# Sample rows in two groups of four and sample state updates four steps behind, in the gated linear attention heads of a two-layer decoder trunk

## The reference

```python
q_dec = q * jnp.exp(bcum); k_state = k * jnp.exp(blast - bcum)
o_intra = jnp.einsum('nbhij,nbhje->nbhie', att, v)
def step(s, inp):
    qc, kc, vc, dc = inp
    o_inter = jnp.einsum('bhid,bhde->bhie', qc, s)
    s = dc[..., None] * s + jnp.einsum('bhjd,bhje->bhde', kc, vc)
    return s, o_inter
...
y = (o * jax.nn.silu(z.astype(F32))).astype(h.dtype) @ w_out      # o after its own RMS norm
```

## Time and profile before

| | |
|---|---|
| runs | 1653.91 us median of 3 (1651.29, 1653.91, 1654.04) |
| profiled execution | span 1651.1 us; no separate time of it is listed, the lowest run is 1651.29 |
| PE busy | 1613.4 us, 98% |
| DVE busy | 818.7 us, 50% |
| ACT busy | 458.2 us, 28% |
| POOL busy | 375.8 us, 23% |
| chain that ended last | PE 94%, DVE 3%, SP's queue, DMA and ACT 1% each |
| mean granted TensorE clock | 0.990 of full speed |

### The profile page before, as it was taken

How to read it: one execution, slowest core, us unless ns; L and a number is a source line. 1 busy time by engine, 2 the same in 40 slices (tenths; PEclk the granted TensorE clock), 3 DMA queues, 4 the chain that set the end, 5 groups by cost and what they waited for, 6 DMA issues and landing times.

```text
span 1651.1 us, 25118 instructions
## 1 busy us (share of the span) xinstructions
PE 1613.4 (98%) x9827; PEld 1501.1 (91%) x9827; DVE 818.7 (50%) x1271; ACT 458.2 (28%) x969; POOL 375.8 (23%) x384
## 2 busy tenths in 40 slices
PE   6999999999999999998999999999999999999996
PEld 5899999999999999998788898888998989979896
DVE  4654449443944475457224562245622356224475
ACT  4321112111211121123325413154040541315423
POOL 3022212211211212211314223133130322314310
PEclk8999999999999999998999999999999999999998
DMA  9512221221122121210202212022120221201312
GB/s 330 193 56 87 62 63 42 84 74 42 55 78 64 57 67 54 77 41 27 64 18 73 84 40 77 13 64 84 53 66 12 64 96 40 77 13 40 110 37 108
DMA packets 137545, 115.03 MB, mean 70 GB/s; under 512 B 6013, under 2 KB 120281, under 8 KB 137442
## 3 DMA queue, kind: packets, MB, share of 16 engines
q1 hardware_dynamic: 135616, 112.87, 22.0%
q10 hardware_dynamic: 1834, 0.74, 0.2%
HBM read 99.05 MB, written 15.00 MB: 69 GB/s over the span
## 4 chain that ended last, share of the span: by engine, by line
PE 94%; DVE 3%; SPq 1%; DMA 1%; ACT 1%; issue 0%; ACTq 0%; DVEq 0%
PE psA L549 40%; PE psB L549 29%; PE psB L1804 8%; PE psA L1804 4%; PE psB L1860 2%; PE psB L1877 2%; PE psX L1842 2%; PE psB L1868 2%; PE psX L1897 1%; DVE a_hi L637 1%; PE psB L1909 1%; PE psX L1720 1%; DMA ada<-in_ada_w 1%; DVE y_rows L1606 0%; PE psB L1910 0%; PE psX L1661 0%
## 5 line engine op out<-in xcount | busy, mean ns | idle before, releaser
L344 POOL TENSOR_TENSOR w_lo<-stage,w_hi 128x1024 fp32r<-128x1024 f32 x100 | 249.7, 2496 | 891.1 <-ACT w_hi L339 891.1
L339 ACT ACTIVATE w_hi<-stage 128x1024 fp32r<-128x1024 f32 x100 | 107.0, 1070 | 433.7 <-PE psB L549 297.6
L549 PE MATMUL psA<-h_hi,w_hi 128*128 128x362 f32 (+1 forms) x864 | 210.9, 349 | 4.1 <-DVE h_lo L453 3.8
L549 PE MATMUL psA<-h_lo,w_hi 128*128 128x362 f32 (+1 forms) x864 | 193.6, 329 | 0.0
L549 PE MATMUL psA<-h_hi,w_lo 128*128 128x362 f32 (+1 forms) x864 | 193.1, 329 | 0.0
L549 PEld LDWEIGHTS psA<-h_hi,w_hi 128*128 128x128 f32 x864 | 151.4, 190 | 27.1 <-issue 21.2
L549 PEld LDWEIGHTS psA<-h_hi,w_lo 128*128 128x128 f32 x864 | 151.5, 190 | 0.0
L549 PEld LDWEIGHTS psA<-h_lo,w_hi 128*128 128x128 f32 x864 | 151.4, 190 | 0.0
L549 PE MATMUL psA<-a_hi,w_hi 128*128 128x362 f32 (+1 forms) x480 | 109.7, 334 | 2.6 <-DVE a_lo L640 1.9
L549 PE MATMUL psB<-h_hi,w_hi 128*128 128x362 f32 (+1 forms) x480 | 109.7, 331 | 0.0
L549 PE MATMUL psB<-h_hi,w_lo 128*128 128x362 f32 (+1 forms) x480 | 107.9, 327 | 0.0
(11 more groups left out here) (345 smaller groups left out, 2790.6 us busy)
## 6 DMA issues: line engine op xcount, KB each, us to landing
stage<-in_gla_w_in SPq DMA_DIRECT2D x40, 512.0 KB, 3.8
stage<-in_pool_w_in SPq DMA_DIRECT2D x32, 512.0 KB, 4.1
ada_stage<-in_ada_w SPq DMA_DIRECT2D x24, 512.0 KB, 3.8
ada<-in_ada_w SPq DMA_DIRECT2D x16, 512.0 KB, 8.4
stage<-in_pool_w_out SPq DMA_DIRECT2D x16, 512.0 KB, 3.4
v<-in_state_gla SPq DMA_DIRECT2D x32, 256.0 KB, 2.6
out_new_gla_sample<-v SPq DMA_DIRECT2D x32, 256.0 KB, 2.1
stage<-in_gla_w_out SPq DMA_DIRECT2D x16, 512.0 KB, 3.7
```

The source lines that it names most:

```text
L339: nc.scalar.activation(slot_hi(plan, j), stage[:, j % 2, :], ACT.Copy).then_inc(lay.hi_done, 1)
L344: nc.gpsimd.tensor_tensor(slot_lo(plan, j), stage[:, j % 2, :], slot_hi(plan, j).bitcast(f32), ALU.subtract).then_inc(lay.lo_done, 1)
L549: last = nc.tensor.matmul(ps[u][:, t, 0:width], weight(w[:, p, :], k), a[:, k, n0:n0 + width], start=(k == 0 and pas == 0), stop=(k == kt ...
```

## The change

The rows of the sample sequences are made four at a time, at s = 4 and s = 8, with all four loads waited for first. `sample_update`, `ks_rows` and `sample_state` of sequence b move from step b+2 to step b+4. Those of the last three sequences leave the scan: on PE they stand behind steps k = 0, 2 and 4 of Z3, on DVE around `gate_product(0)` and `(1)`. `sample_out` is split: its first part stays at s = 9, its second part and the release of the unit stand behind Z3's step 0. The second `mean_square(8)` goes from behind step 1 to behind step 3. Stores follow on SP.

```diff
@@ SP
-                    if s >= 2:
-                        store_state(s - 2)
+                    if 4 <= s <= NSUP:
+                        store_state(s - 4)
+                    if s == NSUP + 1:
+                        for b in range(NB - 3, NB):
+                            store_state(b)
@@ DVE
-                for s in range(NSUP + 2):
-                    if s >= 2:
-                        ks_rows(s - 2)
+                for s in range(NSUP + 1):
+                    if s >= 4:
+                        ks_rows(s - 4)
...
-                    if s >= 2:
-                        sample_state(s - 2)
-
+                    if s >= 4:
+                        sample_state(s - 4)
+
+                ks_rows(NB - 3)
+                sample_state(NB - 3)
+                ks_rows(NB - 2)
+                dve.wait_ge(smp_o_evac, g + 1)
+                gate_product(0)
+                sample_state(NB - 2)
+                ks_rows(NB - 1)
+                gate_product(1)
+                sample_state(NB - 1)
                 dve.wait_ge(s0_ready, (g + 1) * NB)
                 dve.wait_ge(o_evac, (g + 1) * NSUP)
                 dve.sem_inc(L1.evac[1], 1)
-                dve.wait_ge(smp_o_evac, g + 1)
-                gate_product(0)
-                gate_product(1)
                 dve.wait_ge(orms_ready, g + 1)
@@ PE
-                    if s >= 3:
-                        pe.wait_ge(s0_ready, g * NB + s - 2)
+                    if s >= 5:
+                        pe.wait_ge(s0_ready, g * NB + s - 4)
...
-                    for b in (b0, b0 + 1):
+                    for b in range(b0, b0 + 4):
                         pe.wait_ge(s0_loaded[b % 4], g * 32 + (b // 4) * 16 + 16)
+                    for b in range(b0, b0 + 4):
...
-                    if b + 2 < NSUP:
-                        pe.wait_ge(S_ready, g * NSUP + b + 3)
+                    if b + 4 < NSUP:
+                        pe.wait_ge(S_ready, g * NSUP + b + 5)
...
-                    if s in (2, 4, 6, 8):
-                        sample_inter(s - 2)
+                    if s in (4, 8):
+                        sample_inter(s - 4)
+                    if 4 <= s <= NSUP:
+                        sample_update(s - 4)
                     if s == NSUP + 1:
-                        sample_out()
-                    if s >= 2:
-                        sample_update(s - 2)
-                pe.sem_inc(L1.unit_done, 1)
+                        sample_out_att()
...
                 for k in range(KD):
                     last = product_step(GP.slot["Z3"] % 2, GP.set[u], k, KD, w8, h_hi, h_lo)
-                    if k == 1:
+                    if k == 0:
+                        sample_out_rows()
+                        pe.sem_inc(L1.unit_done, 1)
+                    if k in (0, 2, 4):
+                        sample_update(NB - 3 + k // 2)
+                    if k == 3:
                         pe.wait_ge(smp_o_evac, g + 1)
                         mean_square(NSUP)
```

More of the change, by code:

```diff
@@ L1911, in sample_update, with sample_out_att @@
                                      stop=True).then_inc(smp_upd, 1)
-                def sample_out():
+                def sample_out_att():
                     pe.wait_ge(smp_attr, g + 1)
@@ L1921, in sample_out, with sample_out_rows @@
                                              skip_group_check=True)
+                def sample_out_rows():
                     pe.wait_ge(smp_rows_out, g + 1)
```

## The result

The changed kernel takes 1662.42 us, median of 6 runs (1657.13 to 1663.8), against 1653.81 us before (6 runs, 1651.29 to 1656.18). The ratio is 1.0044, with a 95% interval of 1.003 to 1.0058: slower by 8.6 us between the medians, and by 7.3 (5.0 to 9.6) by the ratio. Forecast were 10.8 more, 1664.7, with a range of 1655.5 to 1675. The profiled execution took 1662.81 with a span of 1661.0, 9.9 above the one of before. One of the four executions of experiment 1 took 3754.4 us, more than twice any other here; nothing on record explains it, and it is not counted.

The account below looks back on a forecast made before the run. The prediction took PE, busy for 98% of the span, as the bound. Saved work -8.5, wait +12.9, POOL 0 and clock +6.4 gave +10.8 us: 1664.7 against 1653.9, range 1655.5 to 1675.

Parts of the forecast that it names:

- Work saved on PE, 8.5 us: Sample rows in the scan: four matmuls cost PE no more than two, so two pairs at 1.06 us leave each head.
- the 0.2 us a head that were kept for the moved matmuls: Moved matmuls between products of other types: taken as nothing in the sum, 0.2 us a head kept for the range.
- The hole, 12.9 us: Between NRM and O01: PE waits for Z3's late SiLU, 3.2 us a head, 12.9 in all.
- The clock, 6.4 us: Behind each hole: PE falls to half clock, losing 0, 1.4 or 2.8 us a head; 1.6 taken, 6.4 in all.
- (a): Rival: PE waits between NRM and O01 but its clock stays up; +4.4 us, 1658.3, chance 0.15.
- (b): Rival: w_lo of O01 gets ahead of gate_product(1), PE's wait grows to 4.3 us, clock falls; +17, 1671, chance 0.15.
- (c): Rival: DVE's chain to O01 stays hidden, so all 8.5 us saved are left; 1645.4, chance 0.10.
- (d): Rival: the four rows matmuls do not run side by side, nothing gained and waits remain; 1673, chance 0.02.
- (e): Rival: a PE wait near 2 us with the clock up, both terms cancel, no change; 1653.9, chance 0.08.
- SP, the loads and the stores: Load waits at s = 4 and s = 8 and the later stores on SP: costed at nothing.
- The ends of the range: 1655.5, below (a) by moved matmuls and the best price of four; 1675, (b) with the dearer clock.
- the shares of ACT and DVE in the chain that ended last: Expected profile sign: ACT and DVE have shares in that chain, beside a new PE wait of about 3.2 us, four times.

Follow-up runs that it names:

- experiment 1: The changed kernel with sample rows again in pairs at steps 2, 4, 6 and 8, state updates left where the change put them: 1669.0 us, ratio 1.008.
- Experiment 4: The kernel before with only sequence 7's update moved behind Z3's step 4 and sample_state(7) behind the two gate products: 1669.82 us, ratio 1.0094.
- experiment 2: The changed kernel with Z3's SiLU ahead of high(2), w_hi of O23 behind high(3), and gate_product(3) ahead of low(2): 1646.66 us, ratio 0.9948.
- experiment 8: The changed kernel with Z3's SiLU ahead of high(2) and w_hi of O23 behind high(3) on ACT, DVE's order kept: 1650.26 us, ratio 0.9977.
- experiment 5: The changed kernel with four NRM matmuls issued again ahead of NRM's own, with the same values, to fill PE's wait: 1655.57 us, ratio 1.0009.
- experiment 6: The changed kernel with sequence 7's update behind Z3's step 3 in place of step 4: 1657.97 us, ratio 1.0026.
- experiment 9: The changed kernel with the last update behind Z3's step 3 and w_lo of O01 ahead of POOL's square_sum(8): 1654.61 us, ratio 1.0003.

## Why the prediction was right, point by point

- **Work saved on PE, 8.5 us:** right. A step with four rows matmuls is as long as one with two (1.76 and 1.75), so two pairs at 1.06 leave each head. The periods give back 2.1 to 2.2 us a head, 8.4 to 8.7 in all; of the 0.2 us a head that were kept for the moved matmuls nothing shows.
- **The hole, 12.9 us:** right, place and owner too. 3.2 us a head were forecast, 2.93 measured, 11.7 in all. Most of the difference is in two terms: `sample_state(7)` began 0.67 us after its update, not 0.75, and between its end and the reciprocals were 0.17 us, not 0.41. The 0.41 of before stood ahead of another instruction, `gate_product(0)`, and was carried over without a reason. What it was made of is open; the evacuation of the sample rows, which `gate_product(0)` also waits for, had ended on ACT at 1137.74 (L1203, 0.38 us from 1137.36), before `sample_state(7)` did. Experiment 4 shows that one moved update makes the hole, experiment 2 that it goes through ACT's order, and experiment 8 what DVE's order adds.
- **The clock, 6.4 us:** right in kind, with a chance, and too large. It fell behind all four holes of the changed kernel's profiled execution and behind two in those of experiments 1 and 4, with holes of the same length; each time it cost 1.1 us, 4.3 for four heads. 1.4 of every 3.4 us were forecast from matmul counts, and the 1.6 a head took some dearer cases of 2.8, which no head showed. Part of the 1.4 comes back, because O01's step 3 then has no wait ahead of it, which it has at full clock in experiment 5 (0.20 us, and a slower restart). That it fell four times of four was luck for the forecast: one of the six timed executions, 1657.13 with a mean clock of 0.988, came near (a), 1658.3, though its heads are not on record. Experiment 5 shows the clock as a cost of its own.
- **(b), `w_lo` ahead of `gate_product(1)`:** did not happen. DVE was first and POOL waited, 3.38 us in place of 2.39. That DVE and POOL shut each other out is nevertheless real, and cost 1.0 us of DVE's chain as soon as the chain moved (experiments 6 and 9).
- **(c), faster:** the condition named there, that the SiLU need not stand behind `high(2)`, is what experiment 2 made true, and 1646.66 came of it, where 1645.4 was given. (a) did not happen in full in the profiled execution, (d) and (e) not at all.
- **SP, the loads and the stores** stayed without a wait of PE, as forecast.
- **Readings that were off without bearing on the sum:** the clock in the earlier trace rows shows an 8 in the middle too, at the idle stretch between the layers, not only in the first and last slices. The ends of the range don't quite come out of the terms named for them, which give 1656.1 and 1674.2. And the shares of ACT and DVE in the chain that ended last hardly moved (DVE 3% to 4%, ACT 1% both times), so they were no sign of the hole.

The likeliest was forecast 2.3 us too high: 1.2 too much hole and 2.1 too much clock, and about 1 us the other way that no term of the forecast holds, so the total is a little closer than its terms are.

The experiments point to a version that beats both kernels: the change with the SiLU of Z3 ahead of `high(2)` and `gate_product(3)` ahead of `low(2)`, 1646.66 us.

## What to carry to other kernels

When work moves behind a late point of the bound engine, look for the whole chain that hangs on its last piece, over all engines, and compare it with what the bound engine has queued until it needs the result. Here it had 0.2 us to spare and its head moved by five steps of a product. An in-order engine that holds a table load and a copy ahead of the evacuation of a PSUM set makes that evacuation as late as its own latest input. And a hole in the PE's work is priced with the clock behind it: here holes of 2.4 us cost 1.1 us more in three heads of four and those of 1.4 us in none, so the microsecond between them was worth up to twice its length.

## What the runs showed of the hardware that was not expected

- Holes of the same 2.9 us let the clock fall behind four of four in one execution and behind two of four in two others; those of 2.4 us behind three of four; those of 1.4 us behind none of four. Each time it was low for 3.4 us and cost 1.1 us, where behind the idle stretch between the layers it was low for 6.8 us in the kernel before.
- 2.1 us of matmuls that compute nothing new, put into a wait, kept the clock up in all four heads and made the kernel 6.9 us shorter by the medians; 4.3 of these are the clock by like stretches.
- One `w_lo` (2.4 us on POOL) held a DVE instruction of 0.35 us for 2.53, and one of 1.23 for 2.27, but never the one with its second input in PSUM, 0.75 in all 32 places of before and after.
- The value product, the same work in every head, took 49.8 or 50.2 us at full clock, in one and the same execution; the cause is open.
